# Lists of the first experts from TensorE, one train of table scatters, and a tail with its shuffles moved ahead

## The chip, the cores and the metric

The kernel runs on one core of one Trainium2 chip. The metric is the device time of one execution in microseconds (us). The time before is the median of three executions.

## The reference, cut to what matters

One block of a streaming encoder, on 512 tokens and 16 meta tokens of width 1024: a normalised input goes through one projection, a convolution and a matrix memory, and an output projection (not touched here). Then a router picks 4 of 32 experts for each token, each expert is two matrix products with a clamped gate between, and the weighted results are summed and normalised:

```python
u2 = rms_norm(h, norm_ffn_g[l])
logits = xt @ router_w + router_b
top_val, top_idx = lax.top_k(logits, TOP_K)          # 4 of 32
gates = jax.nn.softmax(top_val, axis=-1)
...
hcat = xb @ w1[e] + b1[e]                            # 1024 -> 2048
h_glu, h_lin = jnp.split(hcat, 2, axis=-1)
act = clip(h_glu) * sigmoid(1.702 * clip(h_glu)) * (clip(h_lin) + 1)
y = act @ w2[e] + b2[e]                              # 1024 -> 1024
...
h = h + sum over the 4 chosen of gate * y
out = rms_norm(h, final_norm_g)[:, N_META:]
```

## The kernel before, in words

**Stages.** Up to about 525 us the projections, the convolution and the memory; 525 to 545 the router and the first lists; then 32 experts of the same length one after another to about 1531; then the tail. Each expert has 96 slots for tokens, three tiles (`TG`) of 32; the 128 partitions are 4 groups (`CG`) of 32, each with a quarter of the width. More than 96 tokens for one expert would mean another pass (`PASSES`); these inputs need one. An expert on TensorE is 192 matmuls (listed in pairs) of its hidden product (L1624) and 192 of its second product (L1653). SP loads its weights in chunks of 2 MB into a ring (`w_ring`), one expert ahead.

**Which rows an expert gets.** VectorE finds for each token and choice its place in the expert's list (`choose`, `first_slots`, `find_slots`) and its table address `dest`. GpSimd scatters the codes (token and choice) as 4-byte pieces to `slot_table` in DRAM: 16 indirect transfers of 128 pieces, four per tile of tokens (`places_out`). Eight of them go ahead of expert 1's gathers, eight behind. The table is read back into `code_of` by four transfers, one per group, and GpSimd makes two lists of it: `piece_of` (which row pieces to gather) and `row_of` (where the results go), first for four experts (`EARLY`), then for all. An expert's rows come by three indirect gathers into `xs` (`request_rows`, `gather`) and are turned by VectorE into `xT` (L2097); its results go by three indirect scatters to `y_rows` (`results_out`). A gather with a turn waits for TensorE's progress in the expert before (`row_turn`).

**The first two experts.** Expert 0's rows don't come from DRAM: `in_slot` is a one-hot matrix (slot by token) and TensorE multiplies it with the rows (`first_rows`, L1567); VectorE turns them to `xT` (L2051). Expert 1's list is a product too: `in_second` with the token numbers (L1612), copied into `piece_now` by 12 small operations on VectorE (L2060). Expert 0's `row_of` and everything of expert 2 and later come from the table.

**GpSimd's order** is written out by hand: eight scatters, expert 1's three gathers, eight scatters, wait for the table, four reads, lists of four experts, results of expert 0, wait until they have landed, gathers of expert 2, all lists, then a loop from expert 1: results of e, gathers of e + 2... one after another, each behind the landing of the results.

**VectorE in the tail.** Biases lie in `bias_turn`; after each expert the block is turned by a shuffle (`turn_biases`, L2101) and its first rows copied out by two more (`first_bias`, L2084, and the second, L2139). In the tail VectorE adds the gathered results tile by tile in the order 3, 2, 1, 0 (L2194), with expert 31's share out of TensorE's products (`add_products`, L2203). ScalarE makes the sums of squares (L1144), GpSimd the roots in two small operations (L613, L614). Tiles 3 and 2 are scaled by ScalarE (L1150) and GpSimd (L815), tiles 1 and 0 by VectorE (L1700); SP stores them.

## Time and profile before

| | |
|---|---|
| time, median of three (lowest to highest) | 1569.45 us (1568.13 to 1570.44) |
| time of the profiled execution | 1571.4 us |
| span of the profiled execution | 1569.7 us |
| TensorE busy | 1535.4 us (98%) |
| VectorE / GpSimd / ScalarE busy | 746.2 / 528.1 / 282.6 us |
| mean granted TensorE clock | 0.995 |
| mean of the DMA over the span | 314 GB/s |

The span runs from the first to the last instruction of the profiled execution; its own time, 1571.4 us, lies 1.7 us around it. Busy shares are averages over stages that have different limits.

### The profile page before, as it was taken

The page shows a single profiled execution, that of the slowest core. Times are in us where ns is not written, and L with a number is a line of the kernel's source. Part 1 is how long each engine was busy: PE and PEld are TensorE (multiplying, and loading weights), DVE is VectorE, ACT ScalarE, POOL GpSimd, SP SyncE. Part 2 cuts the span into 40 slices and gives each one's busy share as a digit, 9 for nine tenths or more (in the row PEclk, how much of TensorE's full clock was granted, in tenths as well). Part 3 has the DMA queues.
Part 4 walks back from the last instruction along what each step waited for, and adds up shares of the span by engine and source line. Part 5 has one row for each costly group of instructions (what it writes and reads, how often), then busy time and mean ns, then how long its engine had stood idle before and what let it go on. Part 6 is the DMA issues. An engine that isn't in the chain of part 4 may idle for free.

```text
span 1569.7 us, 37658 instructions
## 1 busy us (share of the span) xinstructions
PE 1535.4 (98%) x15984; PEld 902.1 (57%) x15984; DVE 746.2 (48%) x1579; ACT 282.6 (18%) x406; POOL 528.1 (34%) x682
## 2 busy tenths in 40 slices
PE   6999999999999999999999999999999999999996
PEld 6998998877889646443344334434443443344334
DVE  4799899115233633443353334334433443353358
ACT  5333133356222300100010001000100100010001
POOL 7333433463334435322222222222223222222225
PEclk9999999999999999999999999999999999999998
DMA  7553144221175389999999999999999999999994
GB/s 221 162 169 127 57 147 121 81 81 54 59 303 218 95 285 426 423 425 426 426 424 424 426 420 426 425 420 424 423 419 424 423 427 419 424 426 424 427 420 195
DMA packets 103539, 492.24 MB, mean 314 GB/s; under 512 B 12309, under 2 KB 70569, under 8 KB 78404
## 3 DMA queue, kind: packets, MB, share of 16 engines
q1 hardware_dynamic: 83732, 463.29, 73.0%
q0 software_dynamic: 10128, 17.25, 3.0%
q10 hardware_dynamic: 9632, 11.03, 2.3%
q8 instruction: 35, 0.57, 0.2%
q14 instruction: 12, 0.10, 0.0%
HBM read 475.46 MB, written 24.87 MB: 319 GB/s over the span
## 4 chain that ended last, share of the span: by engine, by line
PE 93%; DVE 3%; POOL 1%; issue 1%; SPq 1%; ACT 1%; DMA 1%; another core or an unknown queue 0%; DVEq 0%; POOLq 0%; ACTq 0%
PE banks L1624 42%; PE banks L1161 28%; PE banks L1653 20%; DVE h_res L2194 1%; DMA stage<-in_w_in_dram 1%; SPq L464 0%; PE banks L1520 0%; PE banks L1393 0%; POOL w_lo L627 0%; POOL w_lo L636 0%; DVE u L1977 0%; PE banks L1294 0%; SPq L450 0%; ACT w_hi L868 0%; DVE h_res L2203 0%
## 5 line engine op out<-in xcount | busy, mean ns | idle before, releaser
L1624 PE MATMUL banks<-w_ring,xT 128*32 128x512 f32 x6144 | 670.6, 592 | 1.4 <-issue 1.0
L1624 PEld LDWEIGHTS banks<-w_ring,xT 128*32 128x32 f32 x6144 | 216.7, 110 | 434.5 <-issue 420.9
L1653 PE MATMUL banks<-w_ring,actT 128*32 128x256 f32 x6144 | 339.7, 379 | 0.2 <-issue 0.2
L1653 PEld LDWEIGHTS banks<-w_ring,actT 128*32 128x32 f32 x6144 | 210.8, 110 | 135.3 <-issue 18.0
L2118 DVE TENSOR_TENSOR hid<-banks,bias_now 128x512 f32<-128x512 f32 x96 | 63.9, 666 | 470.3 <-PE banks L1624 470.3
L636 POOL TENSOR_TENSOR w_lo<-stage,w_hi 128x2048 fp32r<-128x2048 f32 x38 | 175.4, 4615 | 257.9 <-ACT w_hi L868 257.9
L695 POOL TENSOR_TENSOR carrier<-carrier 1x1 f32<-1x1 f32 x161 | 30.9, 193 | 590.4 <-DVE y_out L2147 404.2
L1135 ACT ACTIVATE sig<-hid 128x256 f32<-128x256 f32 x96 | 40.0, 417 | 905.1 <-DVE hid L2119 905.1
L1161 PE MATMUL banks<-u_hi,w_hi 128*128 128x264 f32 (+1 forms) x528 | 176.7, 335 | 0.9 <-POOL w_lo L627 0.9
L1161 PE MATMUL banks<-u_hi,w_lo 128*128 128x264 f32 (+1 forms) x528 | 175.2, 332 | 0.0
L1161 PE MATMUL banks<-u_lo,w_hi 128*128 128x264 f32 (+1 forms) x528 | 174.8, 331 | 0.0
L1789 DVE SCALAR_TENSOR_TENSOR banks<-conv_in,taps,banks 128x512 f32<-128x512 f32 x224 | 151.1, 747 | 0.1
L704 POOL DMA_INDIRECT xs<-u_rows,piece_now x99 | 105.1, 1062 | 19.3 <-issue 13.9
L1161 PEld LDWEIGHTS banks<-u_hi,w_hi 128*128 128x128 f32 x528 | 99.5, 188 | 11.1 <-POOL w_lo L627 1.1
L1161 PEld LDWEIGHTS banks<-u_lo,w_hi 128*128 128x128 f32 x528 | 99.7, 189 | 10.1
L1161 PEld LDWEIGHTS banks<-u_hi,w_lo 128*128 128x128 f32 x528 | 99.6, 189 | 9.6 <-issue 0.2
L755 POOL DMA_INDIRECT y_rows<-y_out,row_now x93 | 94.9, 1021 | 15.6 <-issue 15.6
L868 ACT ACTIVATE w_hi<-stage 128x2048 fp32r<-128x2048 f32 x40 | 76.4, 1910 | 105.1 <-PE banks L1161 99.0
L2147 DVE TENSOR_TENSOR y_out<-banks,bias_now 128x256 f32<-128x256 f32 x96 | 40.7, 424 | 98.0 <-PE banks L1653 93.5
L2128 DVE TENSOR_TENSOR act_v<-hid,sig 128x256 f32<-128x256 f32 x96 | 59.7, 622 | 3.3
L2131 DVE STREAM_TRANSPOSE actT<-act_v 128x256 f32<-128x256 f32 x96 | 42.8, 445 | 3.3
L2126 DVE SCALAR_TENSOR_TENSOR hid<-hid 128x256 f32<-128x256 f32 x96 | 40.8, 426 | 3.3
(307 smaller groups left out, 1451.0 us busy)
## 6 DMA issues: line engine op xcount, KB each, us to landing
w_ring<-in_expert_w_dram SPq DMA_DIRECT2D x192, 2048.0 KB
stage<-in_w_in_dram SPq DMA_DIRECT2D x20, 1024.0 KB, 5.2
stage<-in_w_in_dram SPq DMA_DIRECT2D x16, 512.0 KB, 5.6
y_rows<-empty_row ACTq DMA_DIRECT2D x8, 1024.0 KB, 4.7
y_in<-y_rows SPq DMA_DIRECT2D x4, 2048.0 KB, 17.4
stage<-in_conv_pw_w_dram SPq DMA_DIRECT2D x4, 1024.0 KB, 5.2
stage<-in_mlstm_out_w_dram SPq DMA_DIRECT2D x4, 1024.0 KB, 5.2
stage<-in_w_out_dram SPq DMA_DIRECT2D x4, 1024.0 KB, 5.5
```

The lines of the kernel that those rows point to most:

```text
L636: nc.gpsimd.tensor_tensor(w_lo[:, s], stage[:, s], w_hi[:, s].bitcast(F32), ALU.subtract).then_inc(w_lo_made[s], 1)
L704: pool.indirect_dma_start(out=xs[:, t], out_offset=None, in_=u2_pieces, in_offset=bass.IndirectOffsetOnAxis(ap=piece_now[:, t:t + 1], axis=0),
L755: pool.indirect_dma_start(out=y_dram, out_offset=bass.IndirectOffsetOnAxis(ap=row_now[:, t:t + 1], axis=0), in_=y_out[:, t], in_offset=Non ...
L868: nc.scalar.activation(w_hi[:, s], stage[:, s], ACT.Copy).then_inc(w_hi_made[s], 1)
L1161: last = nc.tensor.matmul(dst, l, r, start=(k == 0 and n == 0), stop=(k == KT - 1 and n == 2))
L1624: last = nc.tensor.matmul(banks[32 * g:32 * (g + 1), t].rearrange("p (c j) -> p c j", j=128), xT[:, t, k], units, start=k == 0, stop=k == ...
L1653: last = nc.tensor.matmul(banks[32 * g:32 * (g + 1), 3 + t, 0:GRP], actT[:, t, k], w2_ring[k // 4][:, k % 4, GRP * g:GRP * (g + 1)], start ...
L1789: nc.vector.scalar_tensor_tensor(out=to, in0=src, scalar=taps[:, ct, w:w + 1], in1=acc, op0=ALU.mult, op1=ALU.add).then_inc(conv_step, 1)
L2118: own(nc.vector.tensor_tensor(hid[:, t], banks[:, t], bias1, ALU.add))
L2126: own(nc.vector.scalar_tensor_tensor(out=lin, in0=lin, scalar=1.0, in1=hid[:, t, 0:GRP], op0=ALU.add, op1=ALU.mult))
L2128: own(nc.vector.tensor_tensor(act_v[:, t].rearrange("p (c q j) -> p c j q", q=4, j=32), lin.rearrange("p (c j q) -> p c j q", q=4, j=32), ...
L2131: nc.vector.transpose(actT[:, t].rearrange("p k s -> p (k s)"), act_v[:, t]).then_inc(actT_made, 1)
```

## The change

Expert 2's list and expert 0's `row_of` come from TensorE as well: `in_third` (one-hot for expert 2) and `first_code` (each token's code if it chose expert 0) are made by VectorE ahead of the transposes of L2051, and 16 more small matmuls follow those of L1612. VectorE then writes two columns of `piece_of` and one of `row_of` in 24 small operations instead of 12. GpSimd starts with expert 1's gathers, sends all sixteen scatters behind the third of them, scatters expert 0's results and gathers expert 2's rows without the table, and only then reads the table: first the first pass's codes alone, 32 partitions, one transfer; the other passes' codes behind expert 1's results. In the tail the last turn and second bias stand ahead of expert 31, its first bias within it; tile 2 is scaled by VectorE, and the order of the roots and squares follows.

Only changed lines, without the declarations of the new tiles:

```diff
@@ -99,7 +98,7 @@
-SCALED_BY_POOL = (3, 2)
+SCALED_BY_POOL = (3,)
@@ -669,7 +672,8 @@
-            nc.gpsimd.iota(token_no, [[P, TT]], base=0, channel_multiplier=1, allow_small_or_imprecise_dtypes=True)
+            nc.gpsimd.iota(token_no, [[P, TT]], base=-NONE, channel_multiplier=1, allow_small_or_imprecise_dtypes=True)
+            nc.gpsimd.iota(code_no, [[TOPK * P, TT], [1, TOPK]], base=-NONE, channel_multiplier=TOPK, allow_small_or_imprecise_dtypes=True)
@@ -681,8 +685,6 @@
-            for g in range(CG):
-                chain(nc.gpsimd.memset(group_of[32 * g:32 * (g + 1)], float(g)))
@@ -694,7 +696,7 @@
-            def request_rows(turn=None):
+            def request_rows(turn=None, between=None):
@@ -704,49 +706,27 @@
-            def gather(n, copied, turn=None):
+                    if between is not None:
+                        places_out(between[t])
+            def gather(n, copied, turn=None, between=None):
...
-                request_rows(turn)
+                request_rows(turn, between)
...
-            def places_out(i):
-                pool.wait_ge(dest_made, i + 1)
-                for m in range(TOPK * i, TOPK * (i + 1)):
+            def places_out(columns):
+                for m in columns:
+                    pool.wait_ge(dest_made, m // TOPK + 1)
...
-            pool.wait_ge(table_set, 16)
-            for i in range(2):
-                places_out(i)
-            for i in range(TT):
-                pool.wait_ge(u2_stored[i], 16)
-            pool.wait_ge(tables_made, CG * TG)
-            pool.sem_inc(idx_step, 1)
-            request_rows()
-            for i in range(2, TT):
-                places_out(i)
-            pool.wait_ge(table_written, 16 * TT * TOPK)
-            for g in range(CG):
-                pool.dma_start(code_of[32 * g:32 * (g + 1)], table.rearrange("(x j e) o -> j x (e o)", j=32, e=NE)).then_inc(rows_in, 16)
-            pool.wait_ge(rows_in, 16 * CG)
-            def lists_of(codes, tokens, pieces, rows):
-                chain(nc.gpsimd.tensor_scalar(tokens, codes, -1.5, 0.25, ALU.add, ALU.mult))
-                chain(nc.gpsimd.tensor_scalar(tokens, tokens, TO_WHOLE, None, ALU.add))
-                chain(nc.gpsimd.tensor_scalar(tokens, tokens, -TO_WHOLE, None, ALU.add))
-                nc.gpsimd.tensor_scalar(pieces, tokens, float(CG), group_of, ALU.mult, ALU.add)
-                chain(nc.gpsimd.tensor_scalar(rows, codes, float(CG), group_of, ALU.mult, ALU.add))
-            def results_out(n, stored):
+            def results_out(n, stored, meanwhile=None):
@@ -756,24 +736,64 @@
+                if meanwhile is not None:
+                    meanwhile()
...
-            lists_of(code_of[:, 0:TG, 0:EARLY], token_part[:, 0:TG, 0:EARLY], piece_of[:, :, 0:EARLY], row_of[:, :, 0:EARLY])
+            codes_of_slot = table.rearrange("(x j e) o -> j x (e o)", j=32, e=NE)
+            def tokens_of(tokens, codes):
+                chain(nc.gpsimd.tensor_scalar(tokens, codes, -1.5, 0.25, ALU.add, ALU.mult))
+                chain(nc.gpsimd.tensor_scalar(tokens, tokens, TO_WHOLE, None, ALU.add))
+                chain(nc.gpsimd.tensor_scalar(tokens, tokens, -TO_WHOLE, None, ALU.add))
+            def lists_of(g, tokens, codes, pieces, rows):
+                nc.gpsimd.tensor_scalar(pieces, tokens, float(CG), float(g), ALU.mult, ALU.add)
+                chain(nc.gpsimd.tensor_scalar(rows, codes, float(CG), float(g), ALU.mult, ALU.add))
+            def later_codes_in():
+                pool.dma_start(code_of[:, TG:PASSES * TG], codes_of_slot[:, TG:PASSES * TG]).then_inc(rows_in, 16)
+            pool.wait_ge(table_set, 16)
+            for i in range(TT):
+                pool.wait_ge(u2_stored[i], 16)
+            pool.wait_ge(tables_made, CG * TG)
+            gather(1, 1, None, ((), (), range(TT * TOPK)))
+            pool.wait_ge(tables_made, 2 * CG * TG)
...
+            pool.wait_ge(table_written, 16 * TT * TOPK)
+            pool.dma_start(code_of[:, 0:TG], codes_of_slot[:, 0:TG]).then_inc(rows_in, 16)
+            pool.wait_ge(rows_in, 16)
+            tokens_of(token_part[:, 0:TG], code_of[:, 0:TG])
+            for g in range(CG):
+                lists_of(g, token_part[:, 0:TG], code_of[:, 0:TG], piece_of[32 * g:32 * (g + 1), :, 0:NE], row_of[32 * g:32 * (g + 1), :, 0:NE])
+            nc.gpsimd.tensor_copy(row_now, row_of[:, :, 1]).then_inc(idx_step, 1)
+            pool.wait_ge(idx_step, IDX + 3 + TG)
+            results_out(1, 2, later_codes_in)
+            pool.wait_ge(xT_made, 3 * TG)
+            gather(3, IDX + 8 + TG, 3)
+            pool.wait_ge(rows_in, 32)
...
-                lists_of(code_of[:, t::TG], token_part, piece_of[:, t, 0:PASSES * NE].rearrange("p (q e) -> p q e", e=NE),
-                         row_of[:, t, 0:PASSES * NE].rearrange("p (q e) -> p q e", e=NE))
+                tokens_of(token_part[:, 1:PASSES], code_of[:, TG + t::TG])
+                for g in range(CG):
+                    lists_of(g, token_part[:, 1:PASSES], code_of[:, TG + t::TG],
+                             piece_of[32 * g:32 * (g + 1), t, NE:PASSES * NE].rearrange("p (q e) -> p q e", e=NE),
+                             row_of[32 * g:32 * (g + 1), t, NE:PASSES * NE].rearrange("p (q e) -> p q e", e=NE))
...
-            pool.reg_mov(first_expert, 1)
+            pool.reg_mov(first_expert, 2)
@@ -800,22 +820,19 @@
-            def last_root(m):
-                i = TILE_ORDER[2 + m]
-                pool.wait_ge(squared, before + 4 + m + 1)
+            def last_root(m, count):
+                i = TILE_ORDER[m]
+                pool.wait_ge(squared, before + count)
...
-            for m, i in enumerate(TILE_ORDER[:2]):
-                pool.wait_ge(squared, before + m + 1)
-                rstd(P, f_square[:, i:i + 1], f_rstd[:, i:i + 1], D, rstd_made)
+            last_root(0, 1)
+            pool.wait_ge(squared, before + 2)
...
-            for m, i in enumerate(SCALED_BY_POOL):
-                pool.wait_ge(squared, before + 2 + m + 1)
-                nc.gpsimd.tensor_tensor(h_res[:, i], h_res[:, i], last_g, ALU.mult).then_inc(out_made_pool, 1)
-                if m == 0:
-                    last_root(0)
-            last_root(1)
+            i = SCALED_BY_POOL[0]
+            nc.gpsimd.tensor_tensor(h_res[:, i], h_res[:, i], last_g, ALU.mult).then_inc(out_made_pool, 1)
+            for m in range(1, TT):
+                last_root(m, m + 2)
@@ -1145,9 +1162,10 @@
-            for m, i in enumerate(SCALED_BY_POOL):
-                act.wait_ge(rstd_made, CHUNKS + TT + m + 1)
-                nc.scalar.activation(h_res[:, i], h_res[:, i], ACT.Copy, scale=f_rstd[:, i:i + 1]).then_inc(squared, 1)
+                if m == 0:
+                    act.wait_ge(rstd_made, CHUNKS + TT + 1)
+                    i = SCALED_BY_POOL[0]
+                    nc.scalar.activation(h_res[:, i], h_res[:, i], ACT.Copy, scale=f_rstd[:, i:i + 1]).then_inc(squared, 1)
@@ -1611,6 +1629,13 @@
+            pe.wait_ge(in_slot_made, 3 * TT + 1)
+            for i in range(TT):
+                last = nc.tensor.matmul(banks[0:SLOTS, SECOND_BANK, 1:2], in_third[:, i], token_no[:, i:i + 1], start=i == 0, stop=i == TT - 1)
+            last.then_inc(place_mm, 1)
+            for i in range(TT):
+                last = nc.tensor.matmul(banks[0:SLOTS, SECOND_BANK, 2:3], in_slot[:, i], first_code[:, i:i + 1], start=i == 0, stop=i == TT - 1)
+            last.then_inc(place_mm, 1)
@@ -2046,6 +2071,10 @@
+            for i in range(TT):
+                slots_of(in_third, i, 2).then_inc(in_slot_made, 1)
+            chain(nc.vector.scalar_tensor_tensor(out=first_codes, in0=expert_f, scalar=0.0, in1=code_no, op0=ALU.is_equal, op1=ALU.mult))
+            nc.vector.tensor_reduce(first_code, first_codes, axis=AX.X, op=ALU.add).then_inc(in_slot_made, 1)
@@ -2054,11 +2083,13 @@
-            dve.wait_ge(place_mm, TT + 2)
-            for g in range(CG):
-                for t in range(TG):
-                    nc.vector.tensor_scalar(piece_now[32 * g:32 * (g + 1), t:t + 1], banks[32 * t:32 * (t + 1), SECOND_BANK, 0:1],
-                                            float(CG), float(g), ALU.mult, ALU.add).then_inc(tables_made, 1)
+            dve.wait_ge(place_mm, TT + 4)
+            for to, from_cols, at_col in ((piece_of, slice(0, 2), 1), (row_of, slice(2, 3), 0)):
+                for g in range(CG):
+                    for t in range(TG):
+                        nc.vector.tensor_scalar(to[32 * g:32 * (g + 1), t, at_col:at_col + from_cols.stop - from_cols.start],
+                                                banks[32 * t:32 * (t + 1), SECOND_BANK, from_cols],
+                                                float(CG), float(CG * NONE + g), ALU.mult, ALU.add).then_inc(tables_made, 1)
@@ -2096,6 +2127,10 @@
+                def second_bias():
+                    nc.vector.stream_shuffle(bias2, bias_turn[:, 2 * GRP:3 * GRP], [0] * NE).then_inc(bias2_made, 1)
@@ -2110,11 +2145,15 @@
+                    last = between is not None
...
+                            if last:
+                                dve.wait_ge(bias_turned, n + 1)
@@ -2136,13 +2175,16 @@
-                    nc.vector.stream_shuffle(bias2, bias_turn[:, 2 * GRP:3 * GRP], [0] * NE).then_inc(bias2_made, 1)
+                    if between:
+                        first_bias()
+                    else:
+                        second_bias()
...
-                        elif t == 1 and not between:
+                        elif t == 1 and not last:
@@ -2155,6 +2197,7 @@
+                dve.wait_ge(y_made, (q * NE + (NE - 1)) * TG + 1)
@@ -2207,17 +2250,15 @@
+                second_bias()
+                dve.wait_ge(bias2_made, q * NE + NE)
...
+                turn_biases()
...
-                    if m == 0:
-                        turn_biases()
-                    elif m == TT - 2:
-                        dve.wait_ge(bias_turned, q * NE + NE)
-                first_bias()
```

## Rows read from the trace of the kernel before

**Rows 1.** Chain of waits over the span: start us, us, what.

```profile
544.86 13.96 PE banks L1624 x124
...
581.23 20.05 PE banks L1624 x185
...
612.57 20.81 PE banks L1624 x190
...
705.87 20.60 PE banks L1624 x192
...
736.83 20.60 PE banks L1624 x192
```

**Rows 2.** TensorE's matmuls, 530 to 616: start, us, instruction [idle before <-releaser].

```profile
543.39 0.84 PE L1612 MATMUL banks<-token_no,in_second 128*96 128x1 f32 x8 [0.90 <-DVE in_second L2009]
```

**Rows 3.** Timeline of VectorE, 530 to 616, same columns.

```profile
540.61 0.32 DVE L2009 SCALAR_TENSOR_TENSOR in_slot<-slot_no,banks,mask 128x96 f32<-128x96 f32 x1 [3.00 <-remote]
...
542.32 1.01 DVE L2009 SCALAR_TENSOR_TENSOR in_second<-slot_no,banks,mask 128x96 f32<-128x96 f32 x4
543.25 1.10 DVE L2051 STREAM_TRANSPOSE xT<-banks 128x256 f32<-128x256 f32 x3
...
545.76 2.16 DVE L2060 TENSOR_SCALAR piece_now<-banks 32x1 int32<-32x1 f32 x12
...
611.15 1.10 DVE L2097 STREAM_TRANSPOSE xT<-xs 128x256 f32<-128x256 f32 x3 [6.00 <-DMA xs<-u_rows,piece_now]
```

**Rows 4.** Timeline of TensorE's weight loads, 540 to 582, same columns.

```profile
556.90 0.14 PEld L1624 LDWEIGHTS banks<-w_ring,xT 128*32 128x32 f32 x4 [0.29 <-issue]
...
561.80 0.16 PEld L1624 LDWEIGHTS banks<-w_ring,xT 128*32 128x32 f32 x4 [1.25 <-issue]
...
564.65 0.19 PEld L1624 LDWEIGHTS banks<-w_ring,xT 128*32 128x32 f32 x8 [0.59 <-issue]
```

**Rows 5.** Timeline of GpSimd, 530 to 616, same columns.

```profile
534.85 1.17 POOL L722 DMA_INDIRECT slot_table<-code,dest  x1 [4.57 <-DVE dest L2023]
...
553.09 1.03 POOL L722 DMA_INDIRECT slot_table<-code,dest  x1 [0.30 <-issue]
...
562.03 0.96 POOL L722 DMA_INDIRECT slot_table<-code,dest  x1 [0.30 <-issue]
569.74 2.84 POOL L739 DMA_DIRECT2D code_of<-slot_table  x4 [6.76 <-DMA slot_table<-code,dest]
586.36 0.23 POOL L743 TENSOR_SCALAR token_part<-code_of 128x15 f32<-128x15 int32 x1 [13.78 <-DMA code_of<-slot_table]
...
599.70 0.19 POOL L695 TENSOR_TENSOR carrier<-carrier 1x1 f32<-1x1 f32 x1 [6.82 <-DMA y_rows<-y_out,row_now]
```

**Rows 6.** Busy us of PE, PEld, DVE, ACT, POOL; clock, DMA share, GB/s.

```profile
560.00:565.00 5.00, 4.31 (x17) 0.75 (x19) 0.00 (x0) 0.00 (x0) 2.38 (x3) 1.00 1.00 167
```

**Rows 7.** Timeline of VectorE in the tail, 1518 to 1570.

```profile
1526.91 0.69 DVE L2118 TENSOR_TENSOR hid<-banks,bias_now 128x512 f32<-128x512 f32 x1 [7.85 <-PE banks L1624]
...
1536.03 0.45 DVE L2139 STREAM_SHUFFLE bias_now<-bias_turn 128x256 f32<-128x256 f32 x1
...
1536.95 3.92 DVE L2194 SCALAR_TENSOR_TENSOR h_res<-y_in,gate_now,h_res 128x1024 f32<-128x1024 f32 x3
...
1547.64 1.04 DVE L2101 STREAM_SHUFFLE bias_turn<-bias_turn 128x768 f32<-128x768 f32 x1
...
1558.33 0.72 DVE L2084 STREAM_SHUFFLE bias_now<-bias_turn 128x512 f32<-128x512 f32 x1
1559.47 3.28 DVE L1700 SCALAR_TENSOR_TENSOR h_res<-h_res,small,last_g 128x1024 f32<-128x1024 f32 x1 [0.42 <-POOL small L614]
```

**Rows 8.** Timeline of GpSimd in the tail, 1518 to 1570.

```profile
1549.98 1.63 POOL L614 TENSOR_TENSOR small<-small 128x1 f32<-128x1 f32 x1
...
1558.82 0.55 POOL L614 TENSOR_TENSOR small<-small 128x1 f32<-128x1 f32 x1
1559.34 2.34 POOL L815 TENSOR_TENSOR h_res<-h_res,last_g 128x1024 f32<-128x1024 f32 x1
```

More of the change, by code:

```diff
@@ L44 @@
 EPS = 1e-5
-EARLY = 4
 NE = 32
@@ L259, in hybrid_block @@
         no_code = in_stage("no_code", [SLOTS, PASSES * NE], I32)
-        group_of = in_stage("group_of", [P, 1])
         piece_of = in_stage("piece_of", [P, TG, PASSES * NE + 2], I32)
@@ L267, in hybrid_block @@
         xT = in_stage("xT", [P, TG, KT, 32])
-        code_of = at("code_of", [P, PASSES * TG, NE], I32, one_hot_at)
-        token_part = at("token_part", [P, PASSES, NE], F32, one_hot_at + size([P, PASSES * TG, NE]))
+        code_of = at("code_of", [32, PASSES * TG, NE], I32, one_hot_at)
+        token_part = at("token_part", [32, PASSES, NE], F32, one_hot_at + size([P, PASSES * TG, NE]))
         assert size([P, PASSES * (TG + 1), NE]) <= 2 * size([P, TT, TOPK, NE])
```

9 lines of the change are left out of this document (7 added, 2 removed).

## Prediction

> **What bounds the kernel now.** I read the page first, then the chain of waits, then the timelines of one engine each around the two places that the diff touches: the start of the experts (530 to 616 us) and the tail (from 1518 us). Nearly everything is TensorE: the chain of waits gives it 93% of the span, and a steady expert takes 736.83 - 705.87 = 30.96 us of matmuls without a gap [rows 1]. The change alters none of these matmuls, so it can win only where an expert takes longer than that, and at the end. The chain's starts give the sizes: expert 0 takes 581.23 - 544.86 = 36.37 us, so 5.41 too many; expert 1 31.34, so 0.38 too many; experts 2 to 4 together 93.30, so 0.42 too many. From there on nothing is lost.
>
> Four things stand in the stretch that the diff rewrites.
>
> (a) VectorE stands 3.00 us before the fourth in_slot, released by nothing that the profile can name ("remote") [rows 3]. It waits there for TensorE's place counts; the three in_slot before had come without such a wait. All that follows (the lists of expert 1, the transposes, expert 0) is late by it.
>
> (b) Expert 0's weight loads go four by four, 0.14 + 0.29 = 0.43 us per four. Then the same four need 0.16 + 1.25 = 1.41 us, until 564.65, where they are back at the old pace [rows 4]. From the row at 556.90 to that at 564.65 are 7.75 us in which the view lists 24 loads, which at 0.43 per four take 2.6: some 5.2 us lost, which is expert 0's 5.41 nearly whole.
>
> (c) The first two losses fall beside the 4-byte scatters into the slot table: a first train of eight from 534.85, and a second from 553.09 to 562.99 [rows 5]. At 560 to 565 the DMA engines are busy 1.00 of the time and move only 167 GB/s [rows 6]. That the scatters cause the losses is not shown by this: the loads still come at 0.43 per four at 556.90, when three scatters of the second train had been issued [rows 4, 5].
>
> (d) A second chain, on GpSimd, ends at the same place: the table is read back at 569.74 (after 6.76 us of waiting for the last scatter), the lists start at 586.36 (after 13.78 for the reading), expert 0's results have landed at 599.70, only then are expert 2's rows requested, and VectorE turns them at 611.15 to 612.25, having waited 6.00 for them [rows 3, 5]. TensorE starts expert 2 at 612.57 [rows 1]. So here two chains end within half a microsecond, and one shortened alone gives nothing.
>
> **The change, part by part.** *More work before expert 0.* Four in_third at 1.01/4 = 0.25 us each [rows 3] are 1.0; the two small operations for first_code, with a wait for the first, I put at 0.5 (the 32-by-1 ones of the same stretch take 2.16/12 = 0.18, the in_slot ones 0.32 [rows 3]; bounds 0.36 and 0.7). They stand ahead of the transposes at 543.25, so xT is 1.5 later. TensorE's 16 more matmuls are two groups like the one of 0.84 [rows 2]; the first ends before VectorE's next operand is ready, the second while the transposes (1.10) run. They cost nothing beyond the 1.5, and up to 0.84 if the transposes gave no cover. Term: +1.5.
>
> *List operations, 24 for 12.* Twelve write two columns instead of one; at 0.18 each they release GpSimd as before, 1.5 later. The other twelve add 2.16 to VectorE ahead of the gate sums and the first bias. Nothing waits for these until TensorE ends expert 0's first tile some 14 us later. Term: 0.
>
> *The first scatter train, from 534.85, goes* [rows 5]. If it causes (a), 2.8 of the 3.00 go (the in_slot before it follow at about 0.2); if not, nothing. Bounds -3.0 and 0. I take -2.8, since the wait lies in the train and nothing else of the change touches that place.
>
> *Sixteen scatters behind the gathers.* At 1.27 us from start to start (553.09 to 562.03 for seven steps [rows 5]) they last 20 us on GpSimd, from about 552 to 572. Behind them is the scatter of expert 0's results, whose first tile comes some 6 us before that expert's end (581.23 [rows 1], less what is won ahead): covered by some 2 us. What the longer train does to (b) the trace of before cannot say: bounds -5.2 (it goes) and +5.2 (twice the scatters, twice the loss). Middle: 0.
>
> *Expert 2's rows* no longer wait for the table. The results of expert 0 leave by its end, need 599.70 - 586.36 = 13.3 at most from there (with the list operations in it), and the gather is then held by TensorE's own pace. (d) disappears as a bound, with expert 1's 0.38: -0.4 in this execution. Expert 3's rows are late next: reading the table back and its lists must be done before expert 1's results at about 606. Reading took 13.78 with four transfers; now one, begun about 594, with some 19 small operations of 0.3: 606 if it is as long. That can cost a few us of the pace but the rows are needed only at about 636.
>
> *Tail.* turn_biases (1.04) and first_bias (0.72) leave VectorE's last chain; first_bias takes the place of second_bias (0.45), +0.28; the moved ones fit into the 7.85 us idle before 1526.91 [rows 7]. So the last sum ends up to 1.5 earlier; TensorE's products for the last tile start only after those of the tile before, which can hold back half of it. Tile 2's scale, 2.34 on GpSimd beside VectorE's 3.28 [rows 7, 8], becomes a third one on VectorE. Such an operation alone takes about 1.3 (3.92/3 in the products of the same chain [rows 7]), beside GpSimd 3.28. On the other side the last roots no longer queue behind that multiply. Bounds: -2.5 (the shuffles' 1.5, and half of the 2.0 that a scale now loses beside GpSimd) and -0.4 (the 1.5 less one root held up by a scale, 1.63 - 0.55 = 1.1 [rows 8]). I take -1.3, the shuffles' 1.5 with a little lost.
>
> What speaks against that part: the second operation of GpSimd's root takes 1.63 us beside VectorE's products and 0.55 beside its shuffle [rows 7, 8], and the last three roots will now run beside scales. The Trainium skill (GPSIMD Engine Reference, 1. Specifications) says that GpSimd's SBUF interfaces are shared with VectorE, with contention when a VectorE instruction has two SBUF inputs. The trace agrees, 1.63 against 0.55; by the rule each late root that runs beside a scale costs about 1.1, and with one of them on the path the tail gives -0.4; without it, -2.5.
>
> *The sum* against the profiled execution (span 1569.7, time 1571.4): +1.5 - 2.8 + 0 - 0.4 - 1.3 = -3.0, so 1568.4. The median of the runs shown is 1569.45, 1.95 below that execution, so by this sum 1566.4.
>
> **But does the profiled execution stand for the timed ones?** It is slower than the slowest of the three (1570.44), and its two losses are named by no work of this program. Take them out: TensorE would reach expert 2 at 612.57 - 2.8 - 5.2 - 0.4 = 604.2. The GpSimd chain loses only the 2.8 (it hangs on VectorE's lists, not on expert 0's length), so the rows would be turned at 612.25 - 2.8 and expert 2 start at about 609.6, 3.0 before the profiled one: 1568.4 in all, inside the timed runs' 1568.13 to 1570.44. In such runs the list chain is the whole bound, and the change removes it: expert 2 at 604.2 + 1.5 = 605.7 instead of 609.6, -3.9; with the tail -5.2: 1569.45 - 5.2 = 1564.2.
>
> **The rivals.** 0.2% of 1569.45 is 3.1 us, about what a measurement of this kernel can tell from no change.
> 1. *The list chain bounds the timed runs and goes* (forecast, 0.45): 1564.2; with the tail's and the extra work's bounds 1562.9 to 1565.3.
> 2. *TensorE's slow stretch is in the timed runs too and stays* (0.22): -3.0, 1566.4. For it: expert 0's 36.37 is a plain measurement. Against it: 1571.4 lies above all timed runs.
> 3. *The stretch grows by half with the longer train* (0.18): -3.0 + 2.6 = -0.4, 1569.0. The same comes out if the new lists are late and expert 3 waits: the change does not do what it says.
> 4. *Slower: the train doubles the stretch* (0.10): -3.0 + 5.2 = +2.2, 1571.6, and 1574.4 if the 3.00 us have nothing to do with the first train. It decides from a growth of 3.0 on. For it speaks that both losses lie beside scatters, and 167 GB/s at full busy share [rows 6]. Against it: the second train's first scatters held nobody up (0.43 at 556.90 [rows 4]). The Trainium skill (DMA: Bandwidth & Descriptors, Specifications) wants transfers of at least 512 bytes for full rate and says that smaller ones are done as read-modify-write. By that rule the scatters' 4-byte pieces would slow the ring loads beside them; the 167 GB/s agree with it, but 4 and 16 scatters are not told apart there.
> 5. *The stretch is real and goes with the reordering* (0.05): -3.0 - 5.2 = -8.2, 1561.2.
>
> **How the numbers follow.** Time: the first case, 1564.2. Range: down to case 5, up to just under case 4, 1561.2 to 1571.0, which leaves out the worse half of 4 and the tails of the rest. Faster by over 0.2% (under 1566.3): case 1 nearly whole 0.43, nearly half of case 2 0.09, case 5 0.05, together 0.57. Slower (over 1572.6): the worse part of case 4 with a part of what I have not thought of, 0.09. Same: the rest, 0.34.
>
> **What the profile after would show.** Chain of waits: expert 0 starting at about 543.6 if (a) goes (546.4 if not), lasting 31 to 31.5 if the stretch is gone and 36.4 or more if not; expert 2 one steady expert after expert 1. VectorE: before expert 2's transposes no wait for rows that outlasts TensorE. GpSimd: rows of expert 2 requested before the table is read. Tail: VectorE's last scale ending 1.3 earlier against the end of expert 31; roots still at about 1.6 beside scales. Wrong I would be if expert 0 grew, if expert 3 waited for rows, or if the timed runs of before were bound by TensorE and not by the lists.

## The result, and the profile after

The changed kernel takes 1576.41 us in the median of five runs (1575.98 to 1578.12), the kernel before 1569.45: ratio 1.0045, 95% interval [1.0034, 1.0055]. It is slower by 7 us, outside the range. The two profiled spans, 1574.7 and 1569.7 us, differ by 5.0.

The chain of waits of the changed kernel (start us, us, what). Line numbers are those of the new text: L1649 is the hidden product, L1678 the second one.

```profile
540.77 15.19 PE banks L1649 x116
...
565.56 1.31 PE banks L1649 x4
566.88 1.51 issue
...
587.00 0.19 PE banks L1649
...
617.96 0.19 PE banks L1649
...
648.92 0.19 PE banks L1649
```

Expert 0 starts at 540.77 instead of 544.86, 4.1 earlier. It ends at 587.00: 46.23 us instead of the 36.37 of before [rows 1], 9.9 more. Experts 1 and 2 take the steady 30.96. So all that is lost, and more, is lost within expert 0, and some of the chain's pieces there are "issue", where TensorE waited for nothing that the profile shows.

The weight loads of TensorE in that stretch (start, us, instruction, idle before):

```profile
542.66 0.23 PEld L1649 LDWEIGHTS banks<-w_ring,xT 128*32 128x32 f32 x4 [0.63 <-issue]
...
552.79 0.14 PEld L1649 LDWEIGHTS banks<-w_ring,xT 128*32 128x32 f32 x4 [0.29 <-issue]
...
557.75 0.17 PEld L1649 LDWEIGHTS banks<-w_ring,xT 128*32 128x32 f32 x4 [1.26 <-issue]
...
565.56 0.16 PEld L1649 LDWEIGHTS banks<-w_ring,xT 128*32 128x32 f32 x4 [1.29 <-issue]
566.99 0.11 PEld L1649 LDWEIGHTS banks<-w_ring,xT 128*32 128x32 f32 x1 [1.26 <-issue]
...
572.37 0.18 PEld L1649 LDWEIGHTS banks<-w_ring,xT 128*32 128x32 f32 x4 [0.25 <-issue]
```

Against [rows 4]: the normal pace is 0.43 us per four (552.79). The slow one is four or five per 1.4 us at first, as before, and later only one or two (one between 566.99 and 568.40), and it now lasts from about 555 to 571.9, 17 us instead of 7.7. The view lists 34 loads from 554.90 to 571.92; at 0.43 per four they would take 3.7 us, so 13.4 are lost. There is a second loss that before did not have: at 542.66 four loads take 0.23 + 0.63 = 0.86, just double.

Busy time of two windows (PE, PEld, DVE, ACT, POOL; then granted clock, DMA share, GB/s):

```profile
540.00:545.00 5.00, 5.00 (x34) 1.88 (x36) 4.30 (x27) 1.50 (x2) 0.71 (x4) 0.66 0.00 0
...
555.00:560.00 5.00, 4.17 (x18) 0.76 (x17) 0.00 (x0) 0.00 (x0) 3.78 (x5) 1.00 0.03 1
```

The granted clock is 0.66 in the mean of 540 to 545; loads at half speed mean that it stood at the lower of its two levels, 1.2 GHz, for a part of it. In 555 to 560 the clock is whole, and the DMA engines are nearly idle (share 0.03, 1 GB/s), and yet TensorE does 18 matmuls where 48 to 52 are usual. So the stretch is neither the clock nor a crowded DMA: [rows 6], with a share of 1.00, misled me. Within its five us there is this one, in the midst of the slow stretch of before:

```profile
561.00:562.00 1.00, 0.89 (x5) 0.16 (x4) 0.00 (x0) 0.00 (x0) 0.72 (x1) 1.00 0.00 0
```

TensorE gets four loads in it, where nine are usual, while the DMA engines do nothing.

GpSimd around it, and the table behind it:

```profile
549.12 1.03 POOL L726 DMA_INDIRECT slot_table<-code,dest  x1 [0.30 <-issue]
...
568.29 0.96 POOL L726 DMA_INDIRECT slot_table<-code,dest  x1 [0.30 <-issue]
...
601.95 0.67 POOL L775 DMA_DIRECT2D code_of<-slot_table  x1
609.28 0.26 POOL L748 TENSOR_SCALAR token_part<-code_of 32x96 f32<-32x96 int32 x1 [6.65 <-DMA code_of<-slot_table]
```

Sixteen scatters stand 1.28 us apart from 549.12 to 569.25. TensorE's pace returns 2.7 us behind the last. VectorE:

```profile
535.24 0.32 DVE L2034 SCALAR_TENSOR_TENSOR in_slot<-slot_no,banks,mask 128x96 f32<-128x96 f32 x1 [0.20 <-PE banks L1569]
...
537.88 1.02 DVE L2034 SCALAR_TENSOR_TENSOR in_third<-slot_no,banks,mask 128x96 f32<-128x96 f32 x4
538.82 0.17 DVE L2076 SCALAR_TENSOR_TENSOR first_codes<-expert_f,code_no 128x16 f32<-128x16 f32 x1
539.02 0.17 DVE L2077 TENSOR_REDUCE first_code<-first_codes 128x4 f32<-128x16 f32 x1
539.11 1.10 DVE L2080 STREAM_TRANSPOSE xT<-banks 128x256 f32<-128x256 f32 x3
...
580.50 1.06 DVE L2128 STREAM_TRANSPOSE xT<-xs 128x256 f32<-128x256 f32 x3
...
611.45 1.05 DVE L2128 STREAM_TRANSPOSE xT<-xs 128x256 f32<-128x256 f32 x3
```

The 3.00 us wait before the fourth in_slot [rows 3] is 0.20 now. What made it can be seen on TensorE, in two lines of before (line numbers of the old text) and one of the changed kernel:

```profile
537.83 4.66 PE L1567 MATMUL banks<-u,in_slot 128*32 128x256 f32 x48
540.56 0.11 PEld L1567 LDWEIGHTS banks<-u,in_slot 128*32 128x32 f32 x1 [0.58 <-issue]
...
535.26 2.80 PE L1585 MATMUL banks<-u,in_slot 128*32 128x256 f32 x48
```

Before, the 48 matmuls of the first rows took 4.66 us instead of 2.80, their loads coming in steps of about 0.7 us with "issue" as the reason, as in the later stretch, and the place counts stand behind them. On VectorE the added operations lie between the fourth in_slot and the transposes: these start 3.87 after it, before 2.64, so 1.23 more. The rows of expert 1 (580.50), expert 2 (611.45) and expert 3 (642.57) are turned without a wait for them.

The tail, VectorE and then GpSimd:

```profile
1532.44 0.69 DVE L2157 TENSOR_TENSOR hid<-banks,bias_now 128x512 f32<-128x512 f32 x1 [6.38 <-PE banks L1649]
...
1556.92 5.89 DVE L2237 SCALAR_TENSOR_TENSOR h_res<-y_in,gate_now,h_res 128x1024 f32<-128x1024 f32 x3
...
1564.99 1.28 DVE L1725 SCALAR_TENSOR_TENSOR h_res<-h_res,small,last_g 128x1024 f32<-128x1024 f32 x1
1566.98 1.28 DVE L1725 SCALAR_TENSOR_TENSOR h_res<-h_res,small,last_g 128x1024 f32<-128x1024 f32 x1 [0.72 <-POOL small L617]
1568.98 1.41 DVE L1725 SCALAR_TENSOR_TENSOR h_res<-h_res,small,last_g 128x512 f32<-128x512 f32 x2 [0.71 <-POOL small L617]
```

```profile
1557.57 2.84 POOL L833 TENSOR_TENSOR h_res<-h_res,last_g 128x1024 f32<-128x1024 f32 x1 [1.26 <-ACT h_res L1168]
...
1565.21 1.11 POOL L616 TENSOR_SCALAR small<-small 128x1 f32<-128x1 f32 x1 [1.99 <-ACT y_in L1161]
```

Expert 31's first addition stands at 1532.44, 5.53 later than at [rows 7], the end 5.0 later: the tail gave 0.5. GpSimd's multiply at 1557.57 runs beside three of VectorE's sums, which take 5.89 where such a three took 3.92 in [rows 7]; the last two scales wait 0.72 and 0.71 for a root (before 0.42 [rows 7] and 0.72). From expert 31's first addition to the end of the last scale VectorE needs 37.95 us (1532.44 to 1570.39), before 37.98 (1526.91 to 1564.89): its own chain gave nothing, and the 0.5 lies behind it.

### The profile page after: what moved, and what is told of

Its sections match the earlier page's. It is cut to its first block, busy times and chain, and to the rows that moved or that the text cites. A ratio compares the mean times of both kernels' runs of the same rounds, so it can differ in the third digit from the quotient of the medians.

```text
span 1574.7 us, 37713 instructions
## 1 busy us (share of the span) xinstructions
PE 1537.7 (98%) x16000; PEld 1083.3 (69%) x16000; DVE 751.5 (48%) x1598; ACT 281.5 (18%) x405; POOL 530.4 (34%) x701
## 4 chain that ended last, share of the span: by engine, by line
PE 94%; DVE 2%; POOL 1%; issue 1%; SPq 1%; ACT 1%; DMA 1%; DVEq 0%; POOLq 0%; ACTq 0%
PE banks L1649 43%; PE banks L1179 28%; PE banks L1678 20%; DMA stage<-in_w_in_dram 1%; SPq L467 0%; DVE h_res L2237 0%; PE banks L1538 0%; PE banks L1714 0%; PE banks L1411 0%; POOL w_lo L630 0%; POOL w_lo L639 0%; DVE u L2002 0%; PE banks L1312 0%; ACT w_hi L885 0%; SPq L453 0%
## 5 line engine op out<-in xcount | busy, mean ns | idle before, releaser
L1649 PE MATMUL banks<-w_ring,xT 128*32 128x512 f32 x6144 | 697.5, 593 | 6.0 <-issue 5.6
L1649 PEld LDWEIGHTS banks<-w_ring,xT 128*32 128x32 f32 x6144 | 342.7, 110 | 323.9 <-issue 318.8
L1678 PE MATMUL banks<-w_ring,actT 128*32 128x256 f32 x6144 | 360.8, 379 | 0.0
L1678 PEld LDWEIGHTS banks<-w_ring,actT 128*32 128x32 f32 x6144 | 280.4, 110 | 73.4 <-issue 7.0
```

The lines of the kernel that those rows point to most:

```text
L1649: last = nc.tensor.matmul(banks[32 * g:32 * (g + 1), t].rearrange("p (c j) -> p c j", j=128), xT[:, t, k], units, start=k == 0, stop=k == ...
L1678: last = nc.tensor.matmul(banks[32 * g:32 * (g + 1), 3 + t, 0:GRP], actT[:, t, k], w2_ring[k // 4][:, k % 4, GRP * g:GRP * (g + 1)], start ...
```

## Experiments

Theories: A, the scatters hold TensorE up because they are small writes; C, indirect transfers from GpSimd do it, whatever they move, if they come too densely; D, something else of the new order does it. All runs but one (the kernel before with its second train paced) rest on the changed kernel; line numbers are those of each run's own text. The runs that leave the table or a part of it unwritten are single executions and are read up to expert 2 only; the run with pauses is a single execution too.

**Without scatters.**

```diff
-            gather(1, 1, None, ((), (), range(TT * TOPK)))
+            gather(1, 1)
...
-            pool.wait_ge(table_written, 16 * TT * TOPK)
```

> All sixteen table scatters are left out (nothing is written to the table, so experts 3 and later get no rows: only the time up to expert 2 is read). Theory A (the 4-byte scatters hold TensorE up): expert 0 takes 31 to 31.5 us instead of the 46.5 of the changed kernel, and expert 2 starts near 603. Rival D (something else of the new order, the unpaced gathers or the waits, holds TensorE): expert 0 still takes over 40 us.

Chain of waits:

```profile
542.29 22.50 PE banks L1648 x192
...
575.16 20.60 PE banks L1648 x192
```

Expert 0 takes 575.16 - 542.29 = 32.87 us: 30.96 and the 1.9 by which its hidden product, 22.50 instead of 20.60, pays for the clock. D falls. The stretch of the changed kernel is then 46.23 - 32.87 = 13.4 us.

**Reads instead of writes.**

```diff
-                    pool.indirect_dma_start(out=table, out_offset=bass.IndirectOffsetOnAxis(ap=dest[:, m:m + 1], axis=0),
-                                            in_=code[:, m:m + 1], in_offset=None).then_inc(table_written, 16)
+                    pool.indirect_dma_start(out=code[:, m:m + 1], out_offset=None, in_=table,
+                                            in_offset=bass.IndirectOffsetOnAxis(ap=dest[:, m:m + 1], axis=0)).then_inc(table_written, 16)
```

> The sixteen scatters become sixteen gathers of the same 128 pieces of 4 bytes at the same place in GpSimd's order: same count, same size, same instruction, but reading DRAM instead of writing it (the table stays empty, experts 3 and later get no rows: read up to expert 2 only). Theory A (the small writes do it): expert 0 takes 31 to 32 us. Rival C (sixteen indirect transfers from GpSimd in a row do it, whatever they move): expert 0 takes 40 us or more.

One of the sixteen on GpSimd:

```profile
550.70 0.97 POOL L726 DMA_INDIRECT code<-slot_table,dest  x1 [0.30 <-issue]
```

Expert 0 goes from 542.35 to 592.81, 50.46 us, 17.6 more than without. Some 1.3 of these are the clock: it was granted 0.50 in the mean of 570 to 575, when TensorE had been nearly starved, and 19 loads from 573.65 on take 3.28 us where they take 2.04 at the usual pace. Writes to DRAM are not needed for the loss.

**Each entry in a line of its own.**

```diff
+LINE = 16
...
-        table = nc.dram_tensor("slot_table", [PASSES * SLOTS * NE, 1], I32).ap()
+        wide = nc.dram_tensor("slot_table", [PASSES * SLOTS * NE, LINE], I32).ap()
+        table = wide.rearrange("n (w o) -> (n w) o", o=1)
...
+                nc.vector.tensor_scalar(dest[:, TOPK * i:TOPK * (i + 1)], dest[:, TOPK * i:TOPK * (i + 1)], float(LINE), None, ALU.mult).then_inc(dest_made, 1)
```

> Same sixteen scatters of 4-byte pieces, but each table entry has 64 bytes of its own in DRAM, so no two pieces share a line (indices times 16, one small operation more per tile on VectorE, some 1 us; the first pass's codes are read back as single elements; the later passes' codes are read from a part that is not written, which is right for one pass). Theory A1 (writes into the same lines wait for each other in the memory): expert 0 takes 31 to 34 us and the whole is about 1576.4 - 13 = 1563. Rival A2 (any 4-byte write costs the same): expert 0 still takes 44 us or more, whole about 1577.

1580.59 us, ratio 1.0067 [1.0051, 1.0084]; expert 0 543.63 to 591.00, 47.37. Spreading the pieces in DRAM does not help; both forms of theory A are gone.

**Eight scatters back in front.**

```diff
             pool.wait_ge(table_set, 16)
+            places_out(range(8))
...
-            gather(1, 1, None, ((), (), range(TT * TOPK)))
+            gather(1, 1, None, ((), (), range(8, TT * TOPK)))
```

> The changed kernel with eight scatters back ahead of expert 1's gathers, as before; the other eight behind. Theory A: the 3.0 us wait before the fourth in_slot comes back, expert 0 falls from 46.5 to about 36 to 37, whole about 1576.4 - 10 + 3 = 1569. Rival D (the stretch is not from the scatters): expert 0 keeps 46.

1573.46 us, 1.0019 [1.0009, 1.0029]. VectorE:

```profile
539.50 0.32 DVE L2035 SCALAR_TENSOR_TENSOR in_slot<-slot_no,banks,mask 128x96 f32<-128x96 f32 x1 [3.12 <-remote]
```

The wait of 3 us is back with the first train, and expert 0 falls to 39.30 us (545.03 to 584.33). That is 30.96, the 1.9 of the clock and a stretch of 6.4; 36 to 37 and a whole of 1569 were expected, since the clock was not in that sum and the stretch is 1.0 longer than before.

**A quarter of the pieces.**

```diff
-ap=dest[:, m:m + 1], axis=0),
-                                            in_=code[:, m:m + 1]
+ap=dest[0:32, m:m + 1], axis=0),
+                                            in_=code[0:32, m:m + 1]
```

> The sixteen scatters with 32 of the 128 pieces each (three quarters of the table stay empty, so experts 3 and later get few rows: read up to expert 2 only). Same number of instructions, a quarter of the pieces and of the descriptors that GpSimd makes for them. Theory C1 (the descriptors count): expert 0 takes 31 to 34 us. Rival C2 (the transfers count, each with its fixed part): expert 0 stays over 42 us.

```profile
549.57 0.91 POOL L726 DMA_INDIRECT slot_table<-code,dest  x1 [0.30 <-issue]
```

541.22 to 591.50: 50.28 us. With a quarter of the pieces each transfer is shorter on GpSimd (0.86 for most), they follow each other at 1.17, and the loss is 17.4 (again some 1.3 of it the clock, 0.50 in 565 to 575). It goes by transfers, not by pieces.

**Larger pieces.** The gathers of 256 bytes stand where the scatters stood:

```diff
+                    pool.indirect_dma_start(out=selT.rearrange("p t i c -> p (t i c)")[:, 64 * m:64 * (m + 1)], out_offset=None,
+                                            in_=u2_dram.rearrange("n (g c) -> (n g) c", c=64),
+                                            in_offset=bass.IndirectOffsetOnAxis(ap=piece_now[:, 0:1], axis=0),
```

> The sixteen scatters become sixteen gathers of 128 pieces of 256 bytes of the rows, into a tile that is free until the tail (no table, experts 3 and later get no rows: read up to expert 2 only). If the size of a piece mattered (4 bytes as the bad case), expert 0 would take 31 to 34 us. Theory C (indirect transfers in a row, of whatever size): 44 us or more.

```profile
548.76 1.00 POOL L726 DMA_INDIRECT selT<-u_rows,piece_now  x1 [0.31 <-issue]
```

540.39 to 586.65: 46.26 us, 13.4 lost at 1.30 from start to start.

**Pauses.**

```diff
                                             in_=code[:, m:m + 1], in_offset=None).then_inc(table_written, 16)
+                    for _ in range(4):
+                        chain(nc.gpsimd.memset(no_code, NONE))
```

> The changed kernel with some 1.5 us of other work on GpSimd behind each of the sixteen scatters, so that the train lasts about 45 us, to 593, and expert 0's results go out late. Theory C with a rate (the path takes some scatters per time, and a backlog builds up): expert 0 takes 31 to 34 us, expert 2 waits for its rows by some 8 us. Rival (each scatter costs TensorE its share wherever it stands): experts 0 and 1 together still lose some 15 us.

TensorE's matmuls:

```profile
540.74 22.50 PE L1651 MATMUL banks<-w_ring,xT 128*32 128x512 f32 x192
...
573.42 20.79 PE L1651 MATMUL banks<-w_ring,xT 128*32 128x512 f32 x192
...
615.98 4.22 PE L1651 MATMUL banks<-w_ring,xT 128*32 128x512 f32 x20 [10.43 <-DVE xT L2130]
```

The same sixteen scatters at 2.65 us cost TensorE nothing: expert 0 573.42 - 540.74 = 32.68. Expert 2 waits for its rows (10.43), since expert 0's results leave late, as expected. So it is the rate.

**Three parts.**

```diff
+            gather(1, 1)
+            for m in range(6):
+                pool.wait_ge(ring_used[m // 2] if m % 2 else row_turn[m // 2], 1)
+                places_out(range(m, m + 1))
...
+            results_out(0, 1, lambda: places_out(range(6, 10)))
...
             gather(2, 8 + TG, 2)
+            places_out(range(10, TT * TOPK))
```

> All of the change, but the train in three parts: six scatters at the pace of expert 0's matmuls, four while expert 0's results land, six behind expert 2's gathers. By the theory of a rate expert 0 takes 31 to 34 us, expert 1 at most 2 more than 31, and the whole is about 1576.4 - 13 = 1563, under both kernels. If each scatter costs its share wherever it stands, the whole stays above 1573.

1572.93 us, 1.0014 [1.0004, 1.0024]: a miss, though expert 0 is as without scatters (32.87). VectorE before experts 3 and 4:

```profile
637.82 1.10 DVE L2132 STREAM_TRANSPOSE xT<-xs 128x256 f32<-128x256 f32 x3 [5.19 <-DMA xs<-u_rows,piece_now]
...
674.07 1.10 DVE L2132 STREAM_TRANSPOSE xT<-xs 128x256 f32<-128x256 f32 x3 [10.76 <-DMA xs<-u_rows,piece_now]
```

The table is read later, so VectorE waits 5.19 for expert 3's rows; that costs TensorE nothing, expert 3 starts at 639.35, 30.96 after expert 2. The lists of the later passes, all behind expert 3's gathers, then make expert 4's rows late by 10.76 for VectorE: expert 4 starts at 675.31, 35.96 after expert 3, so 5.0 late, and its hidden product takes 22.50 instead of 20.60 behind that wait (granted clock 0.57 in 676 to 680). Expert 1, with the scatters in the landing of the results, loses 2.2. So the chain of lists is the bound again, at expert 4.

**Paced at 2.0 us**, with the later lists in thirds.

```diff
+            for m in range(11):
+                places_out(range(m, m + 1))
+                pause(2)
...
+            results_out(0, 1, lambda: places_out(range(11, TT * TOPK)))
...
+            later_lists(0)
+            for n in (2, 3):
+                nc.gpsimd.tensor_copy(row_now, row_of[:, :, n]).then_inc(idx_step, 1)
+                pool.wait_ge(idx_step, n * IDX + 3 + TG)
+                results_out(n, n + 1)
+                pool.wait_ge(xT_made, (n + 2) * TG)
+                gather(n + 2, n * IDX + 8 + TG, n + 2)
+                later_lists(n - 1)
...
+            pool.reg_mov(first_expert, 4)
```

> All of the change, with some 0.75 us of other GpSimd work behind each of eleven scatters (about 2.0 us from start to start instead of 1.27), the other five while expert 0's results land; the lists of the later passes are made one third each behind the gathers of experts 3, 4 and 5 instead of all behind expert 3's. Theory (a rate of indirect transfers that TensorE's issue can stand lies between 1 per 2.65 and 1 per 1.3 us): if 2.0 us is slow enough, expert 0 takes 31 to 33 us, no expert after it waits, and the whole is that of the run without scatters, about 1564, faster than both kernels. If 2.0 us is still too fast, expert 0 takes 36 us or more and the whole is over 1568.

1564.37 us, 0.996 [0.9948, 0.9973]: faster than both. Chain of waits:

```profile
542.25 22.50 PE banks L1668 x192
...
575.11 21.67 PE banks L1668 x188
...
607.53 0.12 PE banks L1668
```

Expert 0 takes 32.86, as without scatters. Expert 1 takes 32.42, 1.5 too many: the five scatters behind the three of the results, at 1.27, are dense again.

**Bursts.**

```diff
+            for columns, rest in ((range(0, 4), 13), (range(4, 8), 8), (range(8, 11), 0)):
+                places_out(columns)
+                pause(rest)
```

> As z_paced, with the same eleven scatters in the same time, but in bursts of four, four and three at 1.27 us with pauses of some 5 and 3 us between. If a backlog builds up only over some 9 us of back-to-back transfers, no stretch: expert 0 31 to 33, whole about 1564. If each burst costs at once, expert 0 takes 34 to 37 and the whole is 1567 or more.

1567.28 us, 0.9981 [0.9972, 0.9991]. Expert 0 takes 35.60 (541.74 to 577.34), 2.7 lost, expert 1 32.10. Both lie in the second forecast (34 to 37; 1567 or more), but not each burst costs: the first shows one pause of the loads (1.15 us before 555.90, usually 0.24), the second none, and behind the third, with the results' scatters right after it, the loads of 570.1 to 573.0 come in steps of 0.72 instead of 0.43.

**The kernel before, its second train paced.**

```diff
-                places_out(i)
+                places_out(i, 4)
```

> The kernel before with some 1.5 us of other GpSimd work behind each of its last eight scatters, so the table is ready some 12 us later. Expert 0's slow stretch should go (31 to 32 us instead of 36.4). My forecast's step, that the list chain is the bound in before: expert 2 then waits for its rows, about 8 us longer than TensorE needs, and the whole is 1569 to 1577, no faster than before. Rival (TensorE's stretch alone bounded before): the whole is about 1565.

1578.52 us, 1.005 [1.0035, 1.0065]. Experts 0 and 1 are whole (542.42 to 573.40 is 30.98), but VectorE before expert 2:

```profile
616.97 1.10 DVE L2099 STREAM_TRANSPOSE xT<-xs 128x256 f32<-128x256 f32 x3 [19.57 <-DMA xs<-u_rows,piece_now]
```

The rows are 5.8 later than in [rows 3], and the pace won goes into that wait: TensorE could start expert 2 at 573.40 + 30.96 = 604.36 and starts it at 618.21, 13.85 late where about 8 were expected. Its hidden product then takes 23.11 instead of 20.60 (granted clock 0.50 to 0.66 between 608 and 620), and the whole lies 1.5 above the range that was expected. The pauses made the rows some 8.4 later counted from the first scatter (532.27 here, 534.85 before); without them they would still come at about 608.6, 4 us after TensorE is ready. So the chain of lists does bound the kernel before as soon as TensorE is not held up.

**Plain transfers.**

```diff
+                    pool.dma_start(selT.rearrange("p t i c -> p (t i c)")[:, 64 * m:64 * (m + 1)],
+                                   u2_dram[P * (m % TT):P * (m % TT + 1), 64 * m:64 * (m + 1)]).then_inc(table_written, 16)
+                    chain(nc.gpsimd.memset(no_code, NONE))
```

> The sixteen scatters become sixteen plain transfers from GpSimd's queue (128 rows of 256 bytes each, addresses known beforehand, no list), with a short operation of 0.3 us behind each, in the same place (no table, experts 3 and later get no rows: read up to expert 2 only). If any transfer that GpSimd issues holds TensorE up at this rate, expert 0 takes 42 us or more. If it is the indirect ones, whose addresses GpSimd works out, expert 0 takes 31 to 33 us.

```profile
550.04 0.62 POOL L726 DMA_DIRECT2D selT<-u_rows  x1
...
551.23 0.56 POOL L726 DMA_DIRECT2D selT<-u_rows  x1 [0.29 <-POOL no_code L728]
```

541.98 to 575.10: 33.12 us, at 1.11 from start to start, denser than the scatters, and of the 13.4 only 0.25 is left. Of the two kinds only the indirect ones hold TensorE up.

**Two scatters ahead.**

```diff
+            spaced(range(2))
             pool.wait_ge(tables_made, CG * TG)
             gather(1, 1)
+            spaced(range(2, 13))
...
+            results_out(0, 1, lambda: places_out(range(13, TT * TOPK)))
```

> As z_paced, but the first two scatters stand spaced ahead of expert 1's gathers, behind the rows' store, and only three of the last ones in the landing of expert 0's results. By the theory of a rate, expert 1's loss of 1.7 us in z_paced (32.6 instead of 31.0) goes to under 0.5 and nothing new is lost before expert 0, so the whole is about 1563. If scatters ahead of expert 0 hold TensorE's place counts as in the kernel before, expert 0 starts up to 3 us later and the whole is 1565 to 1567.

1562.9 us (1561.6 to 1563.03), 0.9957 [0.9943, 0.9971]: the fastest version. Chain of waits, and VectorE's fourth in_slot:

```profile
542.13 22.50 PE banks L1674 x192
...
575.00 20.60 PE banks L1674 x192
...
605.96 20.60 PE banks L1674 x192
...
636.92 20.60 PE banks L1674 x192
```

```profile
536.56 0.32 DVE L2059 SCALAR_TENSOR_TENSOR in_slot<-slot_no,banks,mask 128x96 f32<-128x96 f32 x1 [0.20 <-PE banks L1594]
```

GpSimd's first scatter:

```profile
538.81 1.16 POOL L726 DMA_INDIRECT slot_table<-code,dest  x1 [10.36 <-DMA u_rows<-u]
```

Experts 1 and 2 take 30.96 each, expert 0 32.87, and nothing new is lost before expert 0. The wait of 0.20 is no test of the first train: the two early scatters start at 538.81 and 541.02, when that in_slot is done.

## Why the prediction was wrong

**The step that failed** is "Sixteen scatters behind the gathers ... bounds -5.2 and +5.2. Middle: 0". Measured, the stretch grew from 5.4 us to 13.4. The upper bound took the loss as proportional to the number of scatters. But the pace falls only some 8 to 9 us after the first transfer of a dense row (the first of the three gathers) and stays low to its end and 1 to 3 us beyond; x_first8, where another train ends 4 us ahead of the gathers, has it after 6.4. Before, the row lasted 14 us (548.95 to 562.99) and the pace was low for the last 6 of them; with sixteen it lasts 24.5 (544.80 to 569.25) and the pace is low for the last 15. Toward its end the pace falls further, too, to one or two loads per 1.4 us. The sum with measured terms: -2.8 for the wait, +1.2 for the work ahead, +1.9 for the clock (below), +8.0 for the stretch, -0.4 for expert 1, -0.5 for the tail: +7.4, against the medians' +7.0. (The profiled spans differ by 5.0 only, because the whole head ran some 2.5 us earlier in the later execution: the first tile's in_slot stands at 530.41 there and at 532.96 in the one of before.)

**The choice of the likeliest case** failed with it: I took the stretch for a matter of the profiled execution, because its time lay above the timed runs. The timed runs of the changed kernel (1575.98 to 1578.12) agree with its profiled one, and w_early2, without a dense row, is 6.75 under before in the timed runs of one session (1562.9 against 1569.65). With a stretch in the timed runs of before, the measured terms give -2.8 + 1.2 + 1.9 - 5.4 - 0.4 - 0.5 = -6.0 for it; without one, the list chain's -3.9 - 0.3 (the extra work 1.2 and not 1.5) + 1.9 - 0.5 = -2.8. So the stretch is most likely in all of them; no timed run shows it directly. Two us between a profile and a median bear no conclusion: as far as can be seen they lie in the head, where the first in_slot stands at 532.96 in the profile of before and between 530.04 and 532.59 in the fourteen others.

**Rival 4 had the place right and the reason wrong.** It named the train that prolongs the stretch, but small writes as the cause, and gave it 0.10. Reads, 256-byte pieces and spread entries lose as much, a quarter of the pieces loses no less, plain transfers of 256 bytes at 1.11 lose nothing. The rule of the Trainium skill (DMA: Bandwidth & Descriptors, Specifications) on transfers under 512 bytes thus does not explain it here: w_direct moves pieces as small as y_big does, and its stretch is gone while that of y_big is whole. That the slow stretch has a time in which the DMA engines idle could not be seen in [rows 6], but a finer view of the same trace shows it (0.00 and 0 GB/s in 561 to 562, above).

**What held.** (a) The wait of 3.00 us belongs to the first train: 0.20 without it, 3.12 with it back. Term -2.8: right, and the place counts were late because TensorE's loads were slow beside that train (4.66 against 2.80). (b) VectorE's work before expert 0: 1.23 instead of 1.5, with the matmuls hidden behind it. (c) The chain of lists: gone as a bound in the changed kernel, and shown as one in z_before_paced. (d) The time without a stretch, forecast 1564.2, was measured as 1564.37 and 1562.9, only with spaced scatters and the later lists in thirds. That it is so near is luck in part: the forecast took 3.9 from a list chain that was most likely not the bound and 1.3 from the tail, and had nothing for the clock, and z_paced itself loses 1.5 in expert 1. (e) The 12 more list operations cost nothing; the table was read back in 6.65 us instead of 13.78.

**The tail** gave 0.5 for 1.3, within its bounds but not where the term had it: the last scale was to end 1.3 earlier after the end of expert 31, and VectorE's chain is as long as before (37.95 against 37.98). The shuffles are gone from it, but one multiply on GpSimd costs three sums some 2 us. That two scales wait for roots is not new. The second operation of the last two roots, forecast at about 1.6 beside scales, takes 0.55; their first takes 1.11 and 1.28. With the sharing that the Trainium skill tells of (GPSIMD Engine Reference, 1. Specifications) the trace agrees, 5.89 against 3.92.

**Not forecast:** the clock. Expert 0's hidden product takes 22.50 instead of 20.60 in the runs whose experts are otherwise whole. My +1.5 for the work ahead of expert 0 should have been 1.2 + 1.9. Waits cost clock as well: behind its wait for rows expert 2's hidden product took 22.67 us in the run with pauses and 23.11 in z_before_paced, expert 4's 22.50 in y_between. Expert 0's start at 540.77, 2.8 before my 543.6, is mostly the earlier head; runs with the same new head start it between 540.39 (y_big) and 542.35 (x_reads).

**Still open:** by what path GpSimd's indirect transfers slow TensorE's issue. The profile names no releaser ("issue", "remote"), and the steps of 0.7 and 1.4 us in which the loads come are not explained. Transfers of instructions don't show it: the changed kernel's trace has one of them between 541 and 555 and none between 555 and 572. It also stays open why the first train's four scatters, the first at 534.85, slow TensorE after some 3 us and not after 8 to 9; no run spaces them out. And whether the lists in thirds were needed besides the spacing was not tried alone: y_between speaks for it, whose expert 4 waits for them.

## What to carry to other kernels

Indirect transfers that GpSimd issues back to back (here every 1.17 to 1.30 us for more than some 8 us) can slow TensorE even when it needs nothing from them; at 2.0 us or more, or as plain transfers, they did not. A move that gathers such transfers into one train should be costed by the length of the train, not by what each of them moves. And where two chains end together, as here TensorE and the lists, a change pays only if it shortens both: before paced was slower, the new order unpaced was slower, both together, with the later lists in thirds, are 0.43% faster.

## What the runs showed of the hardware

- TensorE's loads go at four or five per 1.4 us, later one or two, instead of four per 0.43 under a dense row of indirect transfers, with the clock whole and the DMA engines nearly idle (1 GB/s from 555 to 560).
- The loss does not fall with the pieces: 128 pieces of 4 bytes written 13.4 us, of 256 bytes read 13.4, 32 pieces of 4 bytes written 17.4 (some 1.3 of it the clock).
- The granted clock fell to 0.66 in the mean of 540 to 545, loads at half speed (the lower level, 1.2 GHz, for a part of it), after some 2.7 us in which TensorE had done only the 24 one-column products of the lists. The run with eight scatters in front has the old 3 us wait and these products, and its clock falls just so (0.66 in 545 to 550); the two kernels with only eight of these products, before and z_before_paced, keep 1.00. So the fall goes with the new work ahead of expert 0, of which the 16 added products are TensorE's part; no run takes them out alone. The cost is 1.9 us, still in the fastest version.
